# Two-block decoder layer on one core: S5 states two tokens a step, placed between the mLSTM heads, with the projections in the same block

## The chip, the core and the metric

The kernel runs on one core of a Trainium2 chip. The time is device microseconds (us) from the first to the last instruction of one execution, with what lies around it. Engines: TensorE (PE) does matmuls, VectorE (DVE), ScalarE (ACT) and GpSimd (POOL) do elementwise work, SyncE (SP) issues the DMAs. Each runs its own list of instructions in order, and they wait for each other by semaphores.

## The reference

Two blocks are applied to 256 tokens of width 1024. The first (a hybrid mixer and a gated feed-forward) isn't touched. The second puts 16 meta tokens ahead (272 tokens), and computes, cut to what matters:

```python
xn = rmsnorm(h, norm1_g)
u_s, x_m, z_m, g_s, g_m = split(xn @ w_in)          # 512, 1024, 1024, 1024, 1024 columns
# S5: 32 groups of 16 channels and 64 complex states
a_bar = exp(lam * dt);  b_bar = (a_bar - 1) / lam * b
s[t] = a_bar * s[t-1] + b_bar @ u[t]                # written as an associative scan
y = gelu(real(c @ s) + d * u);  y = y * sigmoid(y @ w_glu + b_glu)
# mLSTM: 4 heads of 256
xc = silu(conv4(x_m));  q, k = blockdiag(xc);  v = blockdiag(x_m)
log_i, log_f = gates(q, k, v)
hm = sum_s(w_ts * (q_t . k_s) * v_s) / max(|den|, exp(-m))     # w_ts = exp of gate sums, s <= t
hm = sigmoid(z_m) * hm;  hm = hm * rsqrt(mean(hm ** 2) + eps) * norm_g + skip * xc
h = h + (sigmoid(g_s) * (y @ w_ssm_out) + sigmoid(g_m) * (hm @ w_ml_out)) @ w_out
```

A retrieval of experts (PEER) and a final norm follow.

## The kernel before

Activations lie as channels on 128 partitions by tokens (T = 256, or TT = 272 with the M = 16 meta tokens). Weights come in blocks of 128 x 1024 (512 KB) through a ring of 8 SBUF slots: SP loads them in the order of `stream` (`load`, line 159), each waiting until PE has counted its slot `used`. `project` (PE) and `evacuate` (ACT or DVE) go through them by PSUM bank: PE waits for `full[slot]` and `drained[bank]`, the reader for `used[slot]`. A weight and its input that need precision are split into a rounded high part and a low part (`part_high` on ACT, line 248; `part_low`, line 252) and take three matmuls (`three`, lines 257 to 259). Others are plain f32 matmuls (line 228). A block (`nc.Block`) ends with all engines waiting for each other.

The middle of the second block is two such blocks, lines 1204 to 1258 and 1308 to 1690.

The first does 12 blocks of projection for u_s and x_m: PE three matmuls by eight chunks each (`product`), ACT the high parts and the reading of the banks (line 1251), DVE the low parts. POOL copies x.

The second goes, by PE's list: 2 z products (a z product is one weight block of the 24 for z_m, g_s and g_m, 8 matmuls of 256 columns, read by ACT, line 1299); v (lines 1609, 1615); 2 z products; q and k (line 1623), which wait for the SiLU of the convolution (DVE lines 1336 to 1340, ACT line 1550); 4 z products; the gate sums (line 1630); 2 z products around the row operations of the gates on DVE (lines 1383 to 1396) and ACT; the four heads; the head norms; then the S5 states.

A head: PE spreads rows of gate sums over partitions (lines 1648, 1649) and forms scores (line 1653) and one z product; DVE adds the columns (lines 1403 to 1407), ACT takes exp, DVE multiplies (1410, 1411); PE forms the weighted sums and denominator (line 1664); DVE divides (lines 1416 to 1420) and counts `head_read`, for which the next head on PE waits. After the four heads DVE multiplies by sigmoid(z) and squares all of them (1423, 1425), PE sums (1670), DVE takes one reciprocal of 1024 columns (1430), ACT its root (1574), and DVE 16 steps of gain and skip (1433, 1435).

The S5 states are 16 groups of 128 complex states by 272 tokens, handled in 8 pairs. A complex recurrence becomes two real ones when the inputs are turned by exp(-i theta t): DVE turns (lines 1448 to 1453), scans with the real factor r (line 1461), and POOL and DVE turn back (lines 1513 to 1521, 1464). PE makes a pair's inputs (line 1696), ACT copies them to SBUF (line 1581), and PE sums the outputs (lines 1685, 1686) with a z product for each pair. The tables cos and sin of theta t are made on POOL by doubling, from one angle (lines 1492 to 1502), through the gate and head stages. The last pairs have part of POOL's work on DVE (`SHARED`). Then y on DVE (line 1472), a sigmoid of all gates (line 1585) and the gelu (line 1590) on ACT end the block. The mix stage (from line 1724 on) follows with its own block; its first weights are loaded ahead by SP, at the end of its list in this block.

## Time and profile before

| | |
|---|---|
| median of 3 runs | 1919.95 us (1916.93 to 1920.94) |
| profiled execution | 1916.86 us, span 1915.1 us |
| busy share | PE 89%, DVE 63%, ACT 41%, POOL 23% |
| mean granted TensorE clock | 0.935 |

The page gives averages over a program with several stages; the change touches the stretch from 623 to 957 us. For such a stretch one reads the busy sums by stage and then the timeline of each engine, where a bracket says how long the engine was idle before an instruction and what ended that. A matmul in f32 appears as two records. A granted clock of 1.0 is 2.4 GHz and of 0.5 is 1.2 GHz; in between it is a mean over the stretch. A z product is 16 records of 256 columns.

### The profile page before, as it was taken

To read this page: it belongs to the slowest core of one execution; us is meant where nothing else is said; L and a number is where in the kernel's file an instruction comes from. 1 tells how busy PE (TensorE), PEld (TensorE's weight loads), DVE (VectorE), ACT (ScalarE), POOL (GpSimd) and SP (SyncE) were. 2 spreads that over 40 slices of the span, in tenths; PEclk is the share of its full clock that TensorE was granted. 3 is DMA by queue.
4 is the path that set the end of the run, shared out by engine and by line. 5 is a ranking of instruction groups with operands and counts; after the bars stand their busy time and mean duration, and the time that the engine had idled before them with its cause. 6 is when DMAs were issued, how large, how long until landed. Compare 5 with 4: busy or idle time off the path is not lost. (4 is left out here: it accounts for less than half of the span.)

```text
span 1915.1 us, 32548 instructions
## 1 busy us (share of the span) xinstructions
PE 1698.7 (89%) x10946; PEld 1514.3 (79%) x10946; DVE 1213.2 (63%) x2250; ACT 781.5 (41%) x1330; POOL 444.1 (23%) x355
## 2 busy tenths in 40 slices
PE   5988999779995887777495999899999999999997
PEld 5967987669995874554285999899999988888886
DVE  4374214667776352379844599877777467777776
ACT  3441113045552342011232455455555555555554
POOL 0020001214441049206572779500000000000000
PEclk9989999889997898787697999999999999999999
DMA  6412224235552521011143467655555776766663
GB/s 229 154 33 89 77 87 156 66 122 184 183 186 72 200 67 55 22 55 66 44 143 100 133 214 214 199 178 177 176 175 180 231 239 232 242 230 230 236 236 131
DMA packets 93698, 289.40 MB, mean 151 GB/s; under 512 B 11328, under 2 KB 27968, under 8 KB 93248
## 3 DMA queue, kind: packets, MB, share of 16 engines
q1 hardware_dynamic: 93200, 287.61, 45.4%
q10 hardware_dynamic: 432, 0.90, 0.2%
q8 instruction: 42, 0.69, 0.1%
q14 instruction: 24, 0.20, 0.0%
HBM read 270.64 MB, written 17.83 MB: 151 GB/s over the span
## 5 line engine op out<-in xcount | busy, mean ns | idle before, releaser
L257 PE MATMUL bank<-arena_parts 128*128 128x256 f32 (+2 forms) x1664 | 482.2, 290 | 62.2 <-DVE ring_parts L252 23.5
L259 PE MATMUL bank<-arena_parts,ring_parts 128*128 128x256 f32 (+1 forms) x1600 | 454.7, 284 | 0.0
L2297 DVE TENSOR_TENSOR ring_parts<-ring,arena_parts 128x512 fp32r<-128x512 f32 x434 | 293.3, 689 | 131.1 <-ACT arena_parts L2117 104.3
L257 PEld LDWEIGHTS bank<-arena_parts 128*128 128x128 f32 x1664 | 319.7, 192 | 67.2 <-issue 20.1
L258 PE MATMUL bank<-h_parts,arena_parts 128*128 128x256 f32 x1152 | 324.1, 281 | 0.0
L259 PEld LDWEIGHTS bank<-arena_parts,ring_parts 128*128 128x128 f32 x1600 | 307.5, 192 | 0.0
L252 POOL TENSOR_TENSOR ring_parts<-ring,arena_parts 128x1024 fp32r<-128x1024 f32 x79 | 208.6, 2657 | 296.8 <-ACT arena_parts L248 242.9
L258 PEld LDWEIGHTS bank<-h_parts,arena_parts 128*128 128x128 f32 x1152 | 218.1, 189 | 0.0
L228 PE MATMUL bank<-h,ring 128*128 128x256 f32 x896 | 213.8, 398 | 1.0 <-PEq L1203 1.0
L2086 PE MATMUL bank<-arena_parts,x_parts 128*128 128x512 f32 x512 | 202.9, 396 | 2.7 <-DVE x_parts L2324 2.7
L228 PEld LDWEIGHTS bank<-h,ring 128*128 128x128 f32 x896 | 177.8, 202 | 33.1 <-issue 7.8
L2088 PE MATMUL bank<-arena_parts,x_parts 128*128 128x512 f32 x512 | 202.7, 396 | 0.0
L2087 PE MATMUL bank<-ring_parts,x_parts 128*128 128x512 f32 x512 | 200.9, 392 | 0.0
L2117 ACT ACTIVATE arena_parts<-ring 128x512 fp32r<-128x512 f32 x217 | 136.5, 629 | 124.1 <-PE bank L2088 96.8
L2114 ACT ACTIVATE arena_parts<-ring 128x512 fp32r<-128x512 f32 x217 | 136.6, 630 | 73.1 <-PE bank L2088 58.7
L258 PE MATMUL bank<-arena_parts 128*128 128x256 f32 (+1 forms) x448 | 130.5, 291 | 0.0
L1016 DVE TENSOR_TENSOR ring_parts<-ring,arena_parts 128x1024 fp32r<-128x1024 f32 x66 | 84.8, 1289 | 51.8 <-ACT arena_parts L1011 47.2
L2086 PEld LDWEIGHTS bank<-arena_parts,x_parts 128*128 128x128 f32 x512 | 95.7, 187 | 25.6 <-DVE ring_parts L2297 2.9
L2087 PEld LDWEIGHTS bank<-ring_parts,x_parts 128*128 128x128 f32 x512 | 96.3, 188 | 23.8
L2088 PEld LDWEIGHTS bank<-arena_parts,x_parts 128*128 128x128 f32 x512 | 95.7, 187 | 24.1
L248 ACT ACTIVATE arena_parts<-ring 128x1024 fp32r<-128x1024 f32 x76 | 79.2, 1053 | 58.0 <-DMA ring<-stream 58.0
L1050 PE MATMUL bank<-arena_parts 128*128 128x256 f32 x352 | 100.3, 285 | 2.9 <-DVEq L1100 2.9
(461 smaller groups left out, 3051.4 us busy)
## 6 DMA issues: line engine op xcount, KB each, us to landing
ring<-stream SPq DMA_DIRECT2D x473, 512.0 KB, 3.5
kept<-arena SPq DMA_DIRECT2D x128, 128.0 KB, 2.1
arena<-kept SPq DMA_DIRECT2D x32, 512.0 KB, 4.5
arena<-first SPq DMA_DIRECT2D x1, 2144.0 KB, 8.1
arena<-second SPq DMA_DIRECT2D x1, 1632.0 KB, 7.2
x<-x_t SPq DMA_DIRECT2D x1, 1024.0 KB, 5.8
out<-arena SPq DMA_DIRECT2D x4, 256.0 KB, 2.1
arena<-last ACTq DMA_DIRECT2D x1, 512.0 KB, 3.4
```

Source lines behind the costliest of these rows:

```text
L228: mm = nc.tensor.matmul(b[:, 0:width], w[:, k, :], h[:, k, lo:lo + width], start=k == 0, stop=k == KT - 1)
L252: ns.tensor_tensor(low[:, s, :], ring[:, s, :], high[:, s, :].bitcast(F32), ALU.subtract)\
L257: nc.tensor.matmul(dst, stationary[0], moving[0], start=first, stop=False)
L258: nc.tensor.matmul(dst, stationary[0], moving[1], start=False, stop=False)
L259: return nc.tensor.matmul(dst, stationary[1], moving[0], start=False, stop=last_one)
L1050: mm(b, high[:, s, w], h_high[:, k, :], start=k == 0, stop=False)
L2086: mm(b, gate_high[:, q % 4, t], expert_high[:, m % 2, w], start=False, stop=False)
L2087: mm(b, gate_high[:, q % 4, t], low[:, s, w], start=False, stop=False)
L2088: ins = mm(b, gate_low[:, q % 4, t], expert_high[:, m % 2, w], start=False, stop=last_one)
L2114: nc.scalar.activation(expert_high[:, m % 2, halves[0]], ring[:, s, halves[0]], ACT.Copy)\
L2117: nc.scalar.activation(expert_high[:, m % 2, halves[1]], ring[:, s, halves[1]], ACT.Copy)\
L2297: v.tensor_tensor(low[:, s, w], ring[:, s, w], expert_high[:, m % 2, w].bitcast(F32), ALU.subtract)\
```

## The change

- **One block.** The projections and what follows share a block. The stream has the columns of x_m ahead of those of u_s. The loops are unrolled, DVE makes a channel's convolution after each low part from the fifth block on, ACT a SiLU from the seventh on.
- **Two tokens a step.** The recurrence runs over pairs of tokens: 136 columns instead of 272, with the factor r squared and the angle doubled. PE forms each pair's input as A B u (first token) + B u (second), accumulated in PSUM, which DVE now reads directly. Outputs of one kind of token are C times the state, of the other C A times the state before plus K0 u, K0 = C B by group. A B, C A and K0 are made once: spread copies of A (PE), products (DVE), transposes of B (PE), 32 small matmuls and four copies for K0. The outputs are written to every second column of bank 1.
- **Tables by sines.** DVE multiplies theta by a ramp of 136, takes whole turns off, and ACT takes sin, and cos as 1 - 2 sin^2 of the half. POOL's doubling goes.
- **Norms folded.** Each head is gated, squared (ACT) and summed (PE) at once, and division and norm become one factor 1 / sqrt(mean(hg^2) + eps den^2), with one reciprocal of 256 columns per head. Gain and skip are applied during the next head.
- **Woven.** Each head holds two pairs of states; POOL turns back all eight pairs apart from one product in DVE. The z products go 2, 1, 2, 1, 1, 1, then two in each head, 2 and 6 at the end, the last eight read by ACT with sigmoid.

The core of the diff:

```diff
+        psum = ctx.enter_context(nc.psum_tensor("psum", [P, 8 * 512], F32))
+        bank = [psum[:, i * 512:(i + 1) * 512] for i in range(8)]
         ident, ones, iota = cst[:, 0:P], cst[:, P:2 * P], cst[:, 2 * P:3 * P]
...
+        def z_bank(g):
+            return g % 2 if g < 8 else 0 if g < 16 else g % 2 * 2
...
-                sp.wait_ge(S("second_in"), 16)
-
-            @block.gpsimd
-            def _(pool):
-                poo.link(nc.gpsimd.tensor_copy(x[:], xin[:, :, M:TT]))
-
...
+                poo.tell(g.tensor_copy(x[:], xin[:, :, M:TT]), x_kept, ONCE + 1)
+                for p in range(PAIRS):
+                    cs, sn = er[:, 2 * p:2 * p + 2, CT - OT - 1:CT], ei[:, 2 * p:2 * p + 2, CT - OT - 1:CT]
+                    zr, zi = zt[:, p % 2, 0:2, CT - OT - 1:CT], zt[:, p % 2, 2:4, CT - OT - 1:CT]
+                    pool.wait_ge(S("z_ready"), p + 1)
+                    if p >= 2:
+                        pool.wait_ge(S("c_done"), p - 1)
+                    so, st = s_out[p % 2], s_tmp[p % 2]
+                    poo.link(g.tensor_tensor(so[:, 0], zr, cs, ALU.mult))
+                    poo.link(g.tensor_tensor(st[:, 0], zi, sn, ALU.mult))
+                    poo.link(g.tensor_tensor(so[:, 0], so[:, 0], st[:, 0], ALU.subtract))
+                    poo.link(g.tensor_tensor(so[:, 1], zr, sn, ALU.mult))
+                    poo.tell(g.tensor_tensor(so[:, 1], so[:, 1], st[:, 1], ALU.add), S("s_ready"), p + 1)
...
+                for n in range(12):
+                    part_low(dve, nc.vector, xn_block, n % 4, split["blocks"] + n + 1)
+                    if n >= 4:
+                        conv(n - 4)
...
+                v.tensor_copy(ramp[:, 0:P], iota)
+                v.tensor_scalar(ramp[:, P:CT], iota[:, 0:CT - P], float(P), None, ALU.add)
+                vec.link(v.tensor_tensor(sm(S_TH2), sm(S_TH), sm(S_TH), ALU.add))
+                vec.link(v.tensor_tensor(ei, ramp.unsqueeze(1).broadcast_to([P, 16, CT]),
+                                         sm(S_TH2).unsqueeze(2).broadcast_to([P, 16, CT]), ALU.mult))
+                turn_k, angle = (t.rearrange("p s t -> p (s t)") for t in (er, ei))
+                vec.link(v.tensor_scalar(turn_k, angle, 1.0 / TWO_PI, 12582912.0, ALU.mult, ALU.add))
+                vec.link(v.tensor_scalar(turn_k, turn_k, 12582912.0, None, ALU.subtract))
+                vec.link(v.scalar_tensor_tensor(angle, turn_k, -6.28125, angle, ALU.mult, ALU.add))
+                vec.link(v.scalar_tensor_tensor(angle, turn_k, -0.0019353071795864769, angle, ALU.mult, ALU.add))
+                vec.tell(v.tensor_scalar(angle, angle, 3.1415925, -3.1415925, ALU.min, ALU.max), table_angles, ONCE + 1)
...
+                def rotate(p):
+                    dve.wait_ge(S("bu_done"), p + 1)
+                    cs, sn = er[:, 2 * p:2 * p + 2, :], ei[:, 2 * p:2 * p + 2, :]
+                    xr, xi = (rot[:, n, :].rearrange("p (s t) -> p s t", s=2) for n in range(2))
+                    q0, q1 = (rt[:, n, :].rearrange("p (s t) -> p s t", s=2) for n in range(2))
+                    v.tensor_tensor(q0, bu_im, sn, ALU.mult)
+                    real = step(v.tensor_tensor(xr, bu_re, cs, ALU.mult))
+                    v.tensor_tensor(q1, bu_re, sn, ALU.mult)
+                    v.tensor_tensor(xi, bu_im, cs, ALU.mult).then_inc(S("bu_turned"), 1)
+                    dve.wait_ge(vec.steps, real)
+                    step(v.tensor_tensor(xr, xr, q0, ALU.add))
+                    dve.wait_ge(S("bu_turned"), p + 1)
+                    vec.link(v.tensor_tensor(xi, xi, q1, ALU.subtract))
+                def scan(p):
+                    if p >= 2:
+                        dve.wait_ge(S("s_ready"), p - 1)
+                    for s in range(2):
+                        r = sm(S_R2)[:, 2 * p + s:2 * p + s + 1].broadcast_to([P, CT])
+                        for c in range(2):
+                            xx = rot[:, c, s * CT:(s + 1) * CT]
+                            ins = v.tensor_tensor_scan(zt[:, p % 2, 2 * c + s, :], r, xx, 0.0, ALU.mult, ALU.add)
+                    vec.link(ins)
+                    vec.tell(v.tensor_tensor(s_tmp[p % 2][:, 1], zt[:, p % 2, 2:4, CT - OT - 1:CT],
+                                             er[:, 2 * p:2 * p + 2, CT - OT - 1:CT], ALU.mult), S("z_ready"), p + 1)
...
+                    if hh:
+                        finish_head(hh - 1)
+                    rotate(2 * hh)
...
+                    scan(2 * hh)
                     dve.wait_ge(S("head_sums"), hh + 1)
...
+                    if hh == 0:
+                        dve.wait_ge(S("z_sigmoid"), 1)
+                    vec.tell(v.tensor_tensor(h_ml[:, 2 * hh:2 * hh + 2, :], b3(4), zsig[:, 2 * hh:2 * hh + 2, :], ALU.mult),
+                             head_gated, ONCE + hh + 1)
+                    vec.link(v.tensor_scalar(rd, bank[5][:, 0:T], -1.0, None, ALU.mult))
+                    vec.link(v.tensor_tensor(rd, rd, bank[5][:, 0:T], ALU.max))
+                    vec.tell(v.tensor_tensor(rd, rd, bank[5][:, T:2 * T], ALU.max), head_den, ONCE + hh + 1)
...
+                    rotate(2 * hh + 1)
+                    scan(2 * hh + 1)
+                    if hh:
+                        finish_y(hh - 1)
+                    dve.wait_ge(squares_den, ONCE + hh + 1)
+                    dve.wait_ge(S("ml_sums"), hh + 1)
+                    vec.tell(v.scalar_tensor_tensor(root_h, bank[4][:, 0:T], 1.0 / T, rd, ALU.mult, ALU.add),
+                             S("head_read"), hh + 1)
+                    vec.tell(v.reciprocal(root_h, root_h), S("ml_inverse"), hh + 1)
+                finish_head(3)
+                finish_y(3)
...
+                act.wait_ge(table_angles, ONCE + 1)
+                cos_t, sin_t = (t.rearrange("p s t -> p (s t)") for t in (er, ei))
+                sca.link(a.activation(cos_t, sin_t, ACT.Sin, scale=0.5))
+                a.activation(sin_t, sin_t, ACT.Sin)
+                sca.link(a.activation(cos_t, cos_t, ACT.Square))
+                sca.tell(a.activation(cos_t, cos_t, ACT.Identity, scale=-2.0, bias=ones[:, 0:1]), S("tables"))
+                z_reads(act, 3)
...
+                    act.wait_ge(head_gated, ONCE + hh + 1)
+                    a.activation(hsq, h_ml[:, 2 * hh:2 * hh + 2, :], ACT.Square).then_inc(S("ml_squares"), 1)
+                    act.wait_ge(head_den, ONCE + hh + 1)
+                    a.activation(rd, rd, ACT.Square, scale=RMS_EPS ** 0.5).then_inc(squares_den, 1)
                     z_reads(act, 1)
+                    act.wait_ge(S("ml_inverse"), hh + 1)
+                    a.activation(root_h, root_h, ACT.Sqrt).then_inc(S("ml_root"), 1)
...
+                z_reads(act, 2, ACT.Sigmoid)
                 for b in range(2):
                     act.wait_ge(drained[b], ev_at.banks[b] + 1)
-                sca.link(a.activation(zg[:, 8:24, :].rearrange("p c t -> p (c t)"),
-                                      zg[:, 8:24, :].rearrange("p c t -> p (c t)"), ACT.Sigmoid))
-
-                nc.scalar.activation(spare[:], ones[:, 0:1], ACT.Gelu_apprx_tanh)
-                act.wait_ge(S("s5_y"), 1)
+                gates_read_first = zg[:, 8:16, :].rearrange("p c t -> p (c t)")
+                sca.link(a.activation(gates_read_first, gates_read_first, ACT.Sigmoid))
+                z_reads(act, 6, ACT.Sigmoid)
...
+                for j in range(16):
+                    c, r = j // 4, slice(32 * (j % 4), 32 * (j % 4) + 32)
+                    dst = bank[4][r, 32 * c:32 * c + 32]
+                    mm(dst, bt_re[:, c, r], c_re[:, j, :], start=True, stop=False)
+                    ins = mm(dst, bt_im[:, c, r], c_im[:, j, :], start=False, stop=True)
+                ins.then_inc(k0_made, 1)
...
+                def inputs(p):
+                    if p:
+                        pe.wait_ge(S("bu_turned"), p)
+                    for s in range(2):
+                        j = 2 * p + s
+                        c, r = j // 4, slice(32 * (j % 4), 32 * (j % 4) + 32)
+                        for k, (b, b_a) in enumerate(((b_re, ab_re), (b_im, ab_im))):
+                            dst = bank[6 + s][:, k * CT:(k + 1) * CT]
+                            mm(dst, b_a[r, c, :], even[r, c, :], start=True, stop=False)
+                            ins = mm(dst, b[r, c, :], odd_[r, c, :], start=False, stop=True)
+                        if s == 0:
+                            turn(pe, ins)
+                    ins.then_inc(S("bu_done"), 1)
+                def outputs(p):
+                    c = p // 2
+                    dst = y_bank.rearrange("p (k s) -> p s k", s=2)
+                    if p % 2 == 0:
+                        if c:
+                            pe.wait_ge(y_taken, ONCE + c)
+                        mm(dst[:, 0, :], k0[:, c, :], even[:, c, M // 2:CT], start=True, stop=False)
+                    pe.wait_ge(S("s_ready"), p + 1)
+                    for s in range(2):
+                        j = 2 * p + s
+                        r = slice(32 * (j % 4), 32 * (j % 4) + 32)
+                        for k, m in enumerate((ca_re, ca_im)):
+                            mm(dst[r, 0, :], m[:, j, :], s_out[p % 2][:, k, s, 0:OT], start=False, stop=k == 1)
+                        for k, m in enumerate((c_re, c_im)):
+                            ins = mm(dst[r, 1, :], m[:, j, :], s_out[p % 2][:, k, s, 1:OT + 1], start=k == 0, stop=k == 1)
+                    ins.then_inc(S("c_done"), 1)
...
+                    inputs(2 * hh)
                     z_products(pe, 1)
...
+                        outputs(2 * hh - 1)
+                    inputs(2 * hh + 1)
+                    z_products(pe, 1)
+                    pe.wait_ge(S("ml_squares"), hh + 1)
+                    for c in range(2):
+                        ins = mm(bank[4][:, 0:T], ones, hsq[:, c, :], start=c == 0, stop=c == 1)
+                    ins.then_inc(S("ml_sums"), 1)
+                    outputs(2 * hh)
...
+                outputs(PAIRS - 1)
+                z_products(pe, 6)
...
+    parts += [_blocks(w_in2[:, 512:1536]), _blocks(w_in2[:, :512])]
```

## Rows read from the trace of the kernel before

**Rows 1.** The page: granted clock in 40 slices; stream loads, us to landing.
```profile
PEclk9989999889997898787697999999999999999999
...
ring<-stream SPq DMA_DIRECT2D x473, 512.0 KB, 3.5
```
**Rows 2.** Stretches: length, then per engine busy us (count), clock, DMA share, GB/s.
```profile
623.00:668.00 45.00, 38.25 (x288) 38.04 (x288) 17.55 (x15) 15.39 (x23) 1.89 (x1) 0.88 0.58 201
668.00:748.50 80.50, 67.73 (x314) 51.20 (x314) 35.02 (x80) 31.47 (x62) 50.39 (x122) 0.92 0.22 72
748.50:823.60 75.10, 62.88 (x219) 42.92 (x220) 23.94 (x40) 5.76 (x15) 31.00 (x34) 0.79 0.09 28
823.60:850.00 26.40, 16.61 (x55) 12.11 (x53) 20.28 (x22) 3.06 (x5) 0.00 (x0) 0.74 0.12 40
850.00:957.00 107.00, 66.64 (x234) 41.26 (x232) 97.60 (x96) 20.31 (x45) 59.21 (x36) 0.72 0.16 59
```
**Rows 3.** Timeline, DVE in the states: start, duration, engine, line, shapes, count.
```profile
851.15 0.73 DVE L1448 TENSOR_TENSOR arena<-arena 128x544 f32<-128x544 f32 x1 [1.51 <-ACT arena L1581]
...
861.53 1.67 DVE L1450 TENSOR_TENSOR arena<-arena 128x544 f32<-128x544 f32 x1
...
868.34 2.57 DVE L1461 TENSOR_TENSOR_SCAN arena<-arena 128x272 f32<-128x272 f32 x4
```
**Rows 4.** Timeline, PE in the states and at the mix stage; idle and releaser in brackets.
```profile
857.10 2.42 PE L1696 MATMUL bank<-arena 32*128 32x272 f32 x8
...
867.78 1.07 PE L1685 MATMUL bank<-arena 128*32 128x256 f32 x4 [4.61 <-POOL arena L1521]
...
930.97 0.63 PE L1685 MATMUL bank<-arena 128*32 128x256 f32 x4 [1.45 <-POOL arena L1521]
931.43 0.61 PE L1686 MATMUL bank<-arena 128*32 128x256 f32 x4
...
957.34 2.90 PE L1738 MATMUL bank<-arena,ring 128*128 128x256 f32 x6 [3.50 <-PEq L1308]
```
**Rows 5.** Timeline, PE and DVE in the second head.
```profile
767.64 1.22 PE L1648 MATMUL bank<-arena 4*128 4x256 f32 x2 [4.01 <-DVE arena L1420]
...
769.64 4.42 PE L1653 MATMUL bank<-arena 128*16 128x256 f32 x12
...
777.58 3.02 PE L1664 MATMUL bank<-arena 128*128 128x256 f32 x12
780.53 1.54 PE L1664 MATMUL bank<-arena,cst 128*128 128x256 f32 x6
...
785.33 0.69 DVE L1420 TENSOR_TENSOR arena<-bank,arena 128x512 f32<-128x512 f32 x1
```
**Rows 6.** Timeline, DVE in the norm stage and ACT at the end.
```profile
833.59 6.55 DVE L1430 RECIPROCAL arena<-arena 128x1024 f32<-128x1024 f32 x1
...
934.95 1.28 ACT L1588 ACT_TABLE_LOAD   x1
...
955.66 1.06 ACT L1590 ACTIVATE arena<-arena 128x1024 f32<-128x1024 f32 x1 [19.21 <-DVE arena L1472]
```
**Rows 7.** Timeline, DVE: a convolution, gate rows, one pass of the norm stage.
```profile
671.75 1.57 DVE L1340 SCALAR_TENSOR_TENSOR arena<-arena,par 128x271 f32<-128x271 f32 x3
...
740.51 1.46 DVE L1391 TENSOR_TENSOR arena<-arena 4x272 f32<-4x272 f32 x1
...
746.26 0.43 DVE L1396 TENSOR_TENSOR arena<-arena 4x272 f32<-4x272 f32 x1
...
825.96 2.29 DVE L1425 TENSOR_TENSOR arena<-arena 128x2048 f32<-128x2048 f32 x1
```
**Rows 8.** Timeline, PE from the block's start to the gates.
```profile
668.27 7.14 PE L228 MATMUL bank<-h,ring 128*128 128x256 f32 x32 [1.00 <-PEq L1203]
...
697.22 9.89 PE L1623 MATMUL bank<-arena,ring 128*128 128x272 f32 x32 [4.45 <-ACT arena L1550]
...
720.85 11.17 PE L1630 MATMUL bank<-arena 128*8 128x272 f32 x48
```

521 lines of the change are left out of this document (229 added, 292 removed).

## Prediction, made from the kernel before alone

> **What bounds the kernel now.** I read the slices of the page first. TensorE (PE) has 6 to 9 tenths almost everywhere, but in slices 14 to 20 the granted clock falls to between 6 and 9 tenths [rows 1]: the second block's middle, which is what the change rewrites. Then the stretches from 623 to 957 us [rows 2], each with its busy sums. The first, 623 to 668, is the 12 projections, bound by PE. In the next three PE is busy for 147 of 182 us at clocks of 0.92, 0.79 and 0.74. The last, 850 to 957, is the S5 states: DVE is busy for 97.60 of 107 us and PE for 66.64, much of that stretched by a clock of 0.72. So PE bounds the start, DVE the end, and hand-overs between engines the middle.
>
> The timelines say why. In the states each DVE product with two SBUF inputs takes 1.67 us, against 0.73 for the one that ran with POOL idle; POOL's own take 1.64 each (59.21 / 36 [rows 2]); the scans (2.57 for four) are not touched [rows 3]. A pair costs DVE 97.6 / 8 = 12.2 us. PE then waits 4.61 us for POOL, and its next products take 1.07 us where those behind 1.45 us took 0.63 [rows 4]. In a head PE waits 4.01 us for DVE; ten records' worth of 256 columns then take 4.42 us [rows 5], 0.44 a record; 32 such records in a row take 7.14 at full clock, 0.215 each with the last one's drain [rows 8]. These are the 1.2 and the 2.4 GHz level; a matmul is two records. In the norm stage one reciprocal of 1024 columns takes 6.55 us, with PE waiting [rows 6].
>
> The sum is a walk in trace time from the end of the projections to the start of the mix stage (957.3), which starts 0.6 us after a gelu of 1.06 us ends at 956.7 [rows 6].
>
> **Part 1, one block with the projections.** PE's 12 projections are unchanged. The x_m columns now come first, so DVE makes the convolutions beside them. One channel is three steps of 1.57 us in all [rows 7] and a shorter one, 2.1 with its gaps, and a low-part subtraction 1.2 (DVE's 17.55 us in 15 operations [rows 2]). That is 3.3 us against PE's 3.0 a block for the last eight; the subtractions fall 2.5 us behind and had over 3 us in hand, so I cost it at nothing. If that cover is missing, PE waits about 1 us. ACT adds a SiLU of 0.35 us a block to some 1.5. The barrier (1.00 us) and the wait for SiLU (4.45 us) go [rows 8]. POOL has only its copy and a memset; SP's queue of loads is the same without a break.
>
> PE: start 667.3; two z products 7.1 (674.4); v products, 10.3 by subtraction in rows 8 (697.22 - 4.45 - 668.27 less twice 7.1); one z 3.5 (688.2); q and k 9.7 (697.9), though they are held some 2 us by ACT's sines, whose reads then come faster; eight new transposes, 16 records of half that width at 0.115, 1.9 (699.8); two z 7.1 (706.9); gates 11.2 [rows 8] (718.1). Before, the gates ended at 732.0: 13.9 us earlier, 10.5 of which is only z products moved behind.
>
> **Part 2, tables by sines.** 81 us of POOL work up to 782 go (50.39 + 31.00 [rows 2]); it did not end last, but of DVE's row operations on 4 x 272 one took 1.46 us beside its long products and one 0.43 beside its short ones [rows 7]. DVE adds six passes over 2176 columns; one of 2048 took 2.29 [rows 7], so at most 2.43 each, 14.6 in all, from 672 to 687; then the sines, 41 small ones and two groups of C products, 14 us, to about 704. It waits for PE until 718, so all this is covered by 14 us. ACT adds four passes; 1024 columns took 1.06 [rows 6], so 2.2 each, from 700 to 709, and delays z reads that PE needs only at 718.
>
> Then, to the heads: copy 0.5, z 3.5 beside it, split 1.2 (722.8); DVE 1.6; ACT two table loads of 1.28 [rows 6] and 1.0 (728.0); DVE's six row operations, now uncontended, 3.4 (731.4). PE meanwhile: z 3.5 (726.3), spreading A 1.9 (728.2), and K0. **K0 is not in the trace**: 32 tiny matmuls, 64 records. Bounds: 0.06 us each (half of an output record's 0.46 / 4 = 0.115, the moving side being an eighth [rows 4]) is 3.8; 0.23 (the gates' narrow records, 11.17 / 48 [rows 8]) is 14.9. I take 0.115, the nearest in shape (32 output columns), 7.4 (735.6). Columns 1.2 and z 3.5 follow (740.3), beside DVE's A*B products, 6 x 0.7. Heads start at 740.5, not 748.5. Gain 8 us; 11.6 or 0.5 at the bounds.
>
> **Part 3, the woven heads.** Per head at full clock PE has: selection 0.43, scores 2.15, inputs of a pair 2.4 [rows 4], z 3.45, selection 0.43, sums 4.45 [rows 5], outputs 1.3, inputs 2.4, z 3.45, squares 0.9, outputs 1.3. Sum 22.7. The widths at 0.215 for 256; the sums are 777.58 to 782.07; an output group is four records of 0.46 twice, and drain. Inputs are 8 matmuls of 136 columns for 4 of 272, the same columns; outputs likewise.
>
> DVE: logs 1.3; norm of the head before 2.1; rotation 2.8 (six of 0.43; four read PSUM, where no slowing shows: 0.69 for 512 columns at 785.33 with one such source [rows 5]); weights 1.1; scans 1.5 and product 0.4 (half of 2.57 and 0.69 with a fixed part); gating and denominator 2.1; rotation and scans again 4.7; y 0.5; reciprocal 1.75 (a quarter of 6.55 [rows 6] and a fixed part) and a multiply 0.5. Sum 18.7, under PE. With three SBUF products per pair stretched by 0.5, 21.7, still under.
>
> What ends last: from the scores' end DVE's logs, ACT's exp behind a table load (2.2), the old norm, the rotation and the weights end at 7.4 us. PE, with inputs and z, is at the wait for them at 6.0: idle 1.4. Sums end at 12.3; DVE's rotation can start at once when the second inputs end at 16; PE's z and squares end at 20.5, but its next outputs wait for `y_taken`, which DVE tells at 21.3: idle 0.8. The reciprocal (to 23.6) and ACT's root lie beside the next scores. So the period is 22.7 + 1.4 + 0.8 and 0.6 for hand-overs: 25.5. A gap of 1.45 us left the clock up in the states; gaps of 4.01 and 4.61 did not [rows 4, 5]. Behind PE's waits for squares and for y stand the next scores; behind DVE's wait for the sums stands the second pair.
>
> Four heads: 102 us, to 842.5. They hold the 75.1 of heads, the 26.4 of norms and the 107 of states of before [rows 2].
>
> **Part 4, the tail.** Two z 7.1, last outputs 1.3, six z 20.7: 871.6, with ACT making sigmoids as it reads. Then a read 0.4, the gelu with its table load, now not ahead, 1.28 + 1.06 [rows 6]: 874.4, and 0.6 for the block's end: 875.0. The mix stage's loads now issue only at 871.6; landing takes 3.5 us [rows 1] and the first of these slots is wanted by ACT 2 us after the stage starts, so nothing or 1 us.
>
> **Sum:** 957.3 - 875.0 = 82.3 us. The profiled execution took 1916.86 (span 1915.1), the median of the runs is 1919.95, 3.1 higher. 1916.9 - 82.3 = 1834.6; on the median 1837.7. I say **1838**. All else is as before.
>
> The Trainium skill, "SBUF — State Buffer", section "Door 1: The DMA port swizzle", says that PSUM has 8-byte cachelines and that any non-contiguous PSUM pattern significantly slows matmuls. The outputs now write every second float of the bank. No row here shows such a write.
>
> **Rivals.**
> (a) *Strided outputs.* Outputs write each second column. As a mechanism of this kernel: all 9.6 us of outputs and K0's quarter double, +10 us, 1848; at four times, +30, 1868. For: no row has it. Against: a record of 256 columns takes four passes' time, so writes come slowly (0.215 us). Chance 0.1.
> (b) *The clock does not hold.* If hand-overs in a head sum to 6 us in one or two gaps, PE pays 4 us of half clock after each, as at [rows 4, 5]: period 32, +26, 1864. It decides once one gap exceeds 4 us. For: ACT has four table switches a head. Against: PE has z products between waits. 0.15.
> (c) *The weave is serial* (the slower side). If each engine waits out the others, a head costs 22.7 + 18.7 + 5.7 of ACT (two table loads 2.6, passes 3.1) = 47, +86, 1924. The point is the wait for weights and the wait for squares: both would have to hold with no second work queued. 0.03; between this and (b) another 0.02 within 0.2%.
> (d) *Better than that:* K0 at its low bound (-3.6) and no idle (-11): 1823. 0.1.
> (e) *The change is no weave at all*, the z products at the end being what PE's gaps held before: then only DVE's halved states (about -45) count, 1875. Against: the PE sum shows it is full. 0.03.
>
> **How the numbers follow.** Forecast 0.57, 1828 to 1852 by K0's bounds and 3 us a head. The range 1820 to 1868 takes in (a), (b) and (d); about 0.1 to 0.2 lies outside. A measurement can tell about 0.2% from no change. Faster 0.95, same 0.02, slower 0.03.
>
> **What would show it.** Right: q and k start near 688, gates end near 718; DVE rows about 0.45 us; heads at 740; four head periods of 25 to 26 us with clock near 1.0 and PE over 90% busy; eight z products after the heads; mix stage at 875. Wrong: K0 over 12 us, outputs over 2 us, a PE gap over 2 us in a head, the clock under 0.9 there, or a mix stage that waits for its weights.

## The result, and the profile after

The changed kernel takes **1824.07 us** (median of four runs, 1822.69 to 1825.87), against 1920.45 (1916.93 to 1921.92) for the kernel before: a ratio of 0.9503, 95% interval 0.9488 to 0.9517. The forecast was 1838, the range 1820 to 1868; the result lies below the 1828 to 1852 that the forecast itself was given, in the part that rival (d) had. The profiled execution took 1822.69 us, its span is 1820.9.

The page of the changed kernel: granted clock in 40 slices, as in [rows 1].
```profile
PEclk8989899889999699899979999999999999999999
```
From 637 to 865 us, slices 15 to 19, it reads 9, 9, 8, 9 and 9 tenths; in the kernel before, slices 16 to 20 had 8, 7, 8, 7 and 6. The 6 of slice 14 (592 to 637) is the norm, which ends with a wait of 12.8 us on PE, and the block's start at 624.5.

The windows of the changed kernel: length, then busy us (count) of PE, PE's weight loads, DVE, ACT, POOL, clock, DMA share, GB/s. They are the projections, the v to gate products, the woven heads and the tail, and answer to [rows 2].
```profile
624.50:662.50 38.00, 37.99 (x289) 38.00 (x290) 27.74 (x43) 14.94 (x25) 0.00 (x0) 0.95 0.53 192
662.50:724.50 62.00, 61.01 (x370) 46.40 (x369) 34.06 (x71) 38.21 (x66) 0.00 (x0) 1.00 0.20 70
724.50:827.70 103.20, 102.12 (x529) 77.79 (x528) 63.16 (x147) 24.37 (x37) 27.73 (x38) 0.93 0.13 46
827.70:860.70 33.00, 29.59 (x146) 25.45 (x145) 3.05 (x6) 9.08 (x14) 1.51 (x3) 1.00 0.40 153
```
PE is busy for 230.7 of 236.2 us. In the kernel before, from its first product (629.0) to the mix stage (957.3), it was busy for 252.1 of 328.3 [rows 2, 4]. So of the 92.1 us that went, 70.7 are PE's idle time, and 21.4 are busy time, since fewer products run at half the clock.

The timeline of the changed kernel: PE from the first z product to the mix stage.
```profile
662.32 7.07 PE L229 MATMUL psum<-h,ring 128*128 128x256 f32 x32
...
681.96 7.50 PE L1670 MATMUL psum<-arena,ring 128*128 128x272 f32 x32
689.30 1.04 PE L1675 MATMUL psum<-cst,arena 128*128 128x128 f32 x8
...
718.36 0.28 PE L1703 MATMUL psum<-arena 128*32 128x32 f32 x7
...
718.99 0.23 PE L1704 MATMUL psum<-arena 128*32 128x32 f32 x3
720.21 0.73 PE L1708 MATMUL psum<-cst,arena 4*16 4x4 f32 x6 [0.99 <-DVE arena L1426]
...
724.52 0.69 PE L1751 MATMUL psum<-arena 4*128 4x256 f32 x2
...
740.58 5.41 PE L229 MATMUL psum<-h,ring 128*128 128x256 f32 x16
...
827.73 7.17 PE L229 MATMUL psum<-h,ring 128*128 128x256 f32 x32
...
860.69 8.83 PE L1821 MATMUL psum<-arena,ring 128*128 128x256 f32 x32 [3.41 <-PEq L1274]
```
The whole of K0 (L1703 and L1704, in turns) lies between 718.36 and 719.2. The heads run from 724.52 to 827.73. The z product at 740.58 took 5.41 us where one at full clock takes 3.72, with no idle time ahead of it: the surprise of this case.

DVE's and POOL's steps in the first head, against [rows 3]:
```profile
731.64 0.43 DVE L1454 TENSOR_TENSOR arena<-arena 128x272 f32<-128x272 f32 x1
...
733.50 1.44 DVE L1466 TENSOR_TENSOR_SCAN arena<-arena 128x136 f32<-128x136 f32 x4
...
735.55 0.73 POOL L1301 TENSOR_TENSOR arena<-arena 128x258 f32<-128x258 f32 x1 [114.66 <-DVE arena L1468]
```
A pair's addition fell from 1.67 us to 0.43: with POOL quiet the kernel before took 0.73 for 544 columns [rows 3], and half the columns make that 0.43. POOL's own products fell from 1.64 to 0.73, with 258 columns instead of 512 and no product of DVE beside them.

### The profile page after: what moved, and what is told of

Read it like the earlier page. It is cut to its first block and busy times, and to the rows that moved or that the text cites. A ratio compares the mean times of both kernels' runs of the same rounds, so it can differ in the third digit from the quotient of the medians.

```text
span 1820.9 us, 32801 instructions
## 1 busy us (share of the span) xinstructions
PE 1677.4 (92%) x11170; PEld 1517.9 (83%) x11170; DVE 1152.2 (63%) x2268; ACT 794.7 (44%) x1326; POOL 333.6 (18%) x205
## 5 line engine op out<-in xcount | busy, mean ns | idle before, releaser
L258 PE MATMUL psum<-arena_parts 128*128 128x256 f32 (+2 forms) x1664 | 483.3, 290 | 59.9 <-DVE ring_parts L253 24.1
L260 PE MATMUL psum<-arena_parts,ring_parts 128*128 128x256 f32 (+1 forms) x1600 | 455.6, 285 | 0.0
L258 PEld LDWEIGHTS psum<-arena_parts 128*128 128x128 f32 x1664 | 320.8, 193 | 64.3 <-issue 29.0
L259 PE MATMUL psum<-h_parts,arena_parts 128*128 128x256 f32 x1152 | 325.2, 282 | 0.0
L260 PEld LDWEIGHTS psum<-arena_parts,ring_parts 128*128 128x128 f32 x1600 | 308.5, 193 | 0.0
L259 PEld LDWEIGHTS psum<-h_parts,arena_parts 128*128 128x128 f32 x1152 | 219.4, 190 | 0.0
L229 PE MATMUL psum<-h,ring 128*128 128x256 f32 x896 | 212.2, 397 | 0.0
L2169 PE MATMUL psum<-arena_parts,x_parts 128*128 128x512 f32 x512 | 202.9, 396 | 2.7 <-DVE x_parts L2407 2.7
L2171 PE MATMUL psum<-arena_parts,x_parts 128*128 128x512 f32 x512 | 202.7, 396 | 0.0
L2170 PE MATMUL psum<-ring_parts,x_parts 128*128 128x512 f32 x512 | 200.9, 392 | 0.0
L2169 PEld LDWEIGHTS psum<-arena_parts,x_parts 128*128 128x128 f32 x512 | 95.7, 187 | 25.9 <-DVE ring_parts L2380 2.9
L2171 PEld LDWEIGHTS psum<-arena_parts,x_parts 128*128 128x128 f32 x512 | 95.7, 187 | 24.1
```

Of the source, the lines that this page charges most:

```text
L229: mm = nc.tensor.matmul(b[:, 0:width], w[:, k, :], h[:, k, lo:lo + width], start=k == 0, stop=k == KT - 1)
L258: nc.tensor.matmul(dst, stationary[0], moving[0], start=first, stop=False)
L259: nc.tensor.matmul(dst, stationary[0], moving[1], start=False, stop=False)
L260: return nc.tensor.matmul(dst, stationary[1], moving[0], start=False, stop=last_one)
L2169: mm(b, gate_high[:, q % 4, t], expert_high[:, m % 2, w], start=False, stop=False)
L2170: mm(b, gate_high[:, q % 4, t], low[:, s, w], start=False, stop=False)
```

## The experiments

The base of each is the changed kernel. "Heads" is the time from the first head's first product to the tail. All the kernels share the code ahead of the block, and its first product falls between 623.52 and 629.64 us in them; where two traces are compared, it is therefore from that product. Behind the mix stage's start the kernels share their code too, and still differ by up to 4 us at one place there (the section on the prediction has it), so the causes are read from the block.

**1. The pairs behind the heads.** Is it the weaving that gained?
```
 for hh in range(4):
-    inputs(2 * hh) ... outputs(2 * hh - 1); inputs(2 * hh + 1) ... outputs(2 * hh)
-z_products(pe, 2); outputs(PAIRS - 1); z_products(pe, 6)
+for p in range(PAIRS):
+    inputs(p); z_products(pe, 1)
+    if p: outputs(p - 1)
+outputs(PAIRS - 1)
```


> The pairs of states come after the four heads instead of inside them; the eight z products of the tail go between them, one to a pair. Every operation is kept. Theory A (PE is the bound, and only its products count once the z products lie between the waits): in a head DVE's logs 1.3, ACT's exponential 1.1 and the weights 1.0 with the old norm's 1.7 stand against one z product of 3.7, so PE waits about 1 us a head; a pair has 7.3 us of PE (2.4 + 3.7 + 1.3) against 4.1 of DVE and 4.0 of POOL, so no wait, but the last pair's chain (rotation 2.1, scans 1.9, POOL 4.0) is open by about 3 us and the gelu stands behind it: in all 5 to 10 us over the changed kernel, 1829 to 1834. Theory B (the weaving itself is what gained, since a pair's chain of DVE and POOL or a head's chain can only be hidden by the other): 4 us of waits at each of the four heads and at pairs, with half clock behind each: 30 us or more over, 1855 and up.

Measured: 1823.99 us (1823.55 to 1825.51), ratio 0.9509 (0.9488 to 0.953). The same as woven. Its windows, PE alone, heads and then pairs:
```profile
725.30:790.90 65.60, 64.22 (x280) 1.00 0.19 64
790.90:861.00 70.10, 68.21 (x395) 0.90 0.24 86
```
PE waits 1.4 us in four heads and 1.9 in eight pairs. From first product to mix stage it is 237.95 us against 236.18. One z product in each wait does all that the weave does. Theory A's mechanism holds; of the 5 to 10 us that it priced, 1.8 show in the block and none in the median.

**2. DVE's state work twice.** Did halving it matter?
```
+v.tensor_tensor(q0, ...) ... (the six steps of rotate once more)
-for s in range(2):
+for again in range(2):
+    for s in range(2):
```


> Each rotation and each scan is made twice, so that DVE has per pair about what states of one token at a time would give it, uncontended: 3.7 us more a pair, 7.4 a head, 30 in all. Theory A (DVE is off the path in the woven heads; its waits in a head sum to about 9 us): 0 to 5 us over the changed kernel, 1824 to 1829, with DVE's waits shorter by some 7 us a head. Theory B (halving DVE's work is what made the weave fit): DVE becomes the bound, 15 to 30 us over, 1839 to 1854.

Measured: 1855.11 us (1848.34 to 1859.82), ratio 0.9676 (0.965 to 0.9703): 31 us over, so theory A falls. (The profiled execution is the fastest of the four, 25.7 over the changed kernel's.) The heads' window:
```profile
725.50:857.70 132.20, 118.30 (x530) 88.06 (x529) 93.35 (x227) 24.37 (x37) 27.80 (x38) 0.82 0.11 36
```
Two of PE's waits in the second head, from the timeline, for the weights (the step at L1509) and for y (L1481):
```profile
763.19 0.69 PE L1772 MATMUL psum<-arena 4*128 4x256 f32 x2 [2.35 <-DVE arena L1509]
...
780.82 0.49 PE L1744 MATMUL psum<-arena 128*128 128x128 f32 x2 [2.41 <-DVE arena L1481]
```
Yet theory B's reason is not what the row shows either: DVE is busy for 93 of 132 us and so is not the bound. PE waits 13.9 us in all, mostly for the weights and for y, ahead of which the rotation stands on DVE, and the clock falls to 0.82. Of 29.0 us in the heads, 12.8 are waits, and 16.2 slower products.

**3. Twice the DVE work, with the pairs behind the heads.** Order or amount? The edits of 1 and 2 together.

> Each rotation and scan is made twice, as before, but with the pairs of states behind the heads instead of inside them. Theory A (the 31 us that twice the DVE work cost in the weave came from its order: the rotation stands ahead of the weights and of y, PE waits 2.4 us there and then runs at half clock): a pair has 7.3 us of PE at full clock, and from its inputs to its outputs lie 10.7 us of PE's other work against a chain of 11.7 (rotation 4.4, scans 3.3, POOL 4.0); about 1 us of wait a pair and 3.7 more at the last: 5 to 15 us over the unwoven kernel, 1829 to 1839. Theory B (DVE's amount of work is what counts, wherever it lies): 25 to 35 us over, 1849 to 1859.

Measured: 1843.56 us (1842.68 to 1845.27), ratio 0.9617 (0.9597 to 0.9636): 19.6 us over the unwoven kernel, between both theories. The pairs' window, PE alone:
```profile
791.40:875.00 83.60, 67.08 (x392) 0.90 0.22 82
```
The last pair's outputs, from the timeline:
```profile
873.13 1.06 PE L1749 MATMUL psum<-arena 128*32 128x128 f32 x4 [7.59 <-POOL arena L1305]
```
PE waits 16.5 us in the pairs against 1.9, 7.59 of them for the last pair. From first product to mix stage the doubling costs 14.2 us here (252.18 against 237.95) and 29.0 in the weave (265.23 against 236.18). So half of what it costs in the block comes with the amount, wherever it lies, and half with its place in the weave; the medians (19.6 of 31) also hold differences behind the mix stage's start. Halved state work did matter, not because DVE was full, but because a pair's chain through DVE and POOL must fit beside PE's products.

**4. z products ahead of the inputs.** Meant for the clock:
```
-inputs(2 * hh); z_products(pe, 1)
+z_products(pe, 1); inputs(2 * hh)
 ...
-inputs(2 * hh + 1); z_products(pe, 1)
+z_products(pe, 1); inputs(2 * hh + 1)
```


> In each head both z products come before the pair's input products instead of behind them. In the changed kernel four of eight z products behind inputs ran at half clock for some 3.5 us with no idle time ahead of them, which cost about 7 us. Theory A (the products with 32 rows are what let the clock fall, whatever follows): all z products take 3.72 us, and the half clock strikes the sums and squares that now follow the inputs; cost about the same 7 us. Theory B (the clock falls with something else, DVE's or POOL's work or a fixed interval): half-clock stretches are found again inside z products. For the time: the rotation ahead of the weights starts 3.5 us later, so PE waits up to 3 us for the weights in each head: 0 to 13 us over the changed kernel, 1824 to 1837.

Measured: 1879.4 us (1878.15 to 1882.27), ratio 0.98 (0.9777 to 0.9822): 55 us over, far outside what either theory gave. The heads' window, PE alone:
```profile
726.30:880.40 154.10, 129.65 (x529) 0.71 0.09 31
```
PE's waits for the weights and for y in the second head:
```profile
771.84 1.21 PE L1765 MATMUL psum<-arena 4*128 4x256 f32 x2 [3.31 <-DVE arena L1502]
...
794.88 0.80 PE L1737 MATMUL psum<-arena 128*128 128x128 f32 x2 [3.56 <-DVE arena L1474]
```
PE waits 24.5 us: 3.3 for each head's weights, as I expected, and 3.4 to 3.7 in three heads for `y_taken`, which I had not seen. Of the 50.9 us that the heads are longer, these waits are 23.4 more than before, and 27.5 are slower products. Both theories on the clock meet a trace with too many gaps to tell them apart.

**5. The same first half, with the weights made before the rotation.**
```
-inputs(2 * hh); z_products(pe, 1)
+z_products(pe, 1); inputs(2 * hh)
 ...
-rotate(2 * hh)
 (DVE's two weights steps)
+rotate(2 * hh)
```


> In the first half of each head the z product comes ahead of the pair's inputs, as in the kernel that put z first, but DVE makes the head's weights ahead of the rotation; the second half stays. Theory A (what cost 55 us there were the waits for weights and for y that a later rotation made, and the half clock behind them): no wait for the weights, since they are ready 5.5 us after the scores against 6.0 of PE's own work; 0 to 4 us under the changed kernel, 1820 to 1824, by fewer half-clock stretches. Theory B (a z product ahead of the inputs is itself what hurts): 15 us or more over, 1839 and up.

Measured: 1843.64 us (1842.91 to 1843.93), ratio 0.9614 (0.9595 to 0.9633): 19.6 us over. The heads' window, PE alone, then the second head in pieces:
```profile
725.40:846.40 121.00, 120.26 (x529) 0.75 0.13 40
...
760.00:762.00 2.00, 1.94 (x18) 1.00 0.44 137
762.00:764.00 2.00, 2.00 (x9) 0.58 0.34 133
764.00:766.00 2.00, 2.00 (x6) 0.50 0.00 0
...
780.00:782.00 2.00, 2.00 (x6) 0.50 0.00 0
782.00:784.00 2.00, 2.00 (x9) 0.80 0.00 0
```
The waits are gone (0.7 us in 121), as theory A said, and still it loses 17.8 us in the heads. None of it is waiting, so what is left is the clock: from 762.3 to 782.8 PE works without a gap at 1.2 GHz. It falls just behind the inputs at 759.66, in the sums: 5.39 us where 3.02 is full clock.

**6. No states.**

> The states are left out of the weave: no input products, rotation, scans, POOL products, outputs or sum y; the tables and scaled matrices are still made, and gelu takes what the projections left. Theory A (the states cost what PE's products of them take, 3.7 us a pair, and the half clock behind them): a head falls from 25.8 us to about 16, with PE waiting under 1 us for weights; 8 x 3.7 and 7 us of clock, 37 us under the changed kernel, 1787. Theory B (the states lie in gaps that the heads leave anyway): 10 us or less under. If the half-clock stretches come with the 32-row products, none is left in the heads.

Measured: 1788.08 us (1787.33 to 1789.14), ratio 0.9321 (0.93 to 0.9341): 36 us under, theory A's 37. The heads, PE alone:
```profile
729.60:795.50 65.90, 64.52 (x281) 1.00 0.19 64
```
103.2 - 65.9 = 37.3 us. The work of DVE and POOL on the states is hidden; that of PE is not: the states cost what PE needs for them, and the half clock. The clock is 1.00 throughout.

**7. Inputs on all rows.** The cause of the clock:
```
-mm(dst, b_a[r, c, :], even[r, c, :], start=True, stop=False)
-ins = mm(dst, b[r, c, :], odd_[r, c, :], start=False, stop=True)
+mm(dst, b_a[:, c, :], even[:, c, :], start=True, stop=False)
+ins = mm(dst, b[:, c, :], odd_[:, c, :], start=False, stop=True)
```


> The input products take all 128 rows of the weights and of the moving side instead of one group of 32, with the same columns and count; the sum then runs over four groups, so the states computed are not the reference's. Theory A (products on 32 of the 128 rows are what lets the granted clock fall while PE is never idle): every z product behind inputs takes 3.72 us, none 5.41; 7 us less, 1817. Theory B (the clock falls with PE's columns or with something outside PE): episodes at half clock as before, 1824.

Measured: 1820.91 us (1819.4 to 1821.16), ratio 0.9492 (0.9469 to 0.9515), whose interval overlaps the changed kernel's. The trace is clear where the time isn't; the heads' window, PE alone:
```profile
726.50:823.90 97.40, 94.20 (x530) 1.00 0.16 49
```
The clock is 1.00 in all the heads, though PE is idle for 3.2 us there instead of 1.1, and no z product takes over 3.62. Heads: 97.4 against 103.2. Of these 5.8 us, 2.35 are lost behind the mix stage's start, where its first products took 9.94 us instead of 8.83 and the next 5.41 instead of 3.72. Theory A holds for the cause, and some of the gain is given back later. What changed is the form of the products: whether it is the rows at work or something else that comes with 32-row products can't be told from this, but the zeros of the last kernel below show that it isn't the data.

**8. POOL busy as before.**
```
+for _ in range(24):
+    poo.link(g.tensor_tensor(st, so, so, ALU.mult))
```


> POOL makes 24 products of 516 columns that nobody reads, from 684 us on, where the kernel before made its tables by doubling. Two of 258 columns take 0.73 us each with DVE quiet, so 24 of 516 take some 35 to 40 us and end near the heads' start (724). Theory A (POOL's work slows DVE's products with two SBUF sources, and of those the gate rows and the A*B products lie on the path): the gate rows' two-source steps go from 0.43 to 1.46 us, the last two A*B products from 0.69 to 1.6; the C products slow too but are hidden in DVE's wait of 12.6 us; heads start 3 to 5 us later: 1827 to 1829. Theory B (the slow steps of before had another cause): nothing moves, 1824.

Measured: 1824.39 us (1821.15 to 1826.27), ratio 0.9516 (0.9493 to 0.9539): no change. POOL, then two of DVE's C products, then a gate row, from the timeline:
```profile
683.98 31.10 POOL L1298 TENSOR_TENSOR arena<-arena 128x516 f32<-128x516 f32 x24
...
693.56 1.53 DVE L1404 TENSOR_TENSOR arena<-arena 128x512 f32<-128x512 f32 x1
695.01 1.53 DVE L1405 TENSOR_TENSOR arena<-arena 128x512 f32<-128x512 f32 x1
...
716.90 0.43 DVE L1426 TENSOR_TENSOR arena<-arena 4x272 f32<-4x272 f32 x1
```
A C product takes 0.68 us with POOL quiet and 1.53 beside it, all hidden in DVE's wait of 12.6 us for the gates. The load ended at 715.1, before the gate rows, so theory A's price on the path wasn't tried, and my estimate of when POOL ends was 9 us late. What is shown is that POOL's company is enough for the factor of 2.3 in [rows 3] (1.67 against 0.73): here it is 2.25.

**9. Convolutions after the projections.**
```
     part_low(...)
-    if n >= 4:
-        conv(n - 4)
+for n in range(8):
+    conv(n)
```


> DVE makes the eight convolutions after the last low part instead of beside the projections, and ACT its SiLUs beside the v products; there is still one block. Theory A (what made the front shorter is the order of the products, v ahead of q and k, and the convolutions would have been in time anyway): they end at about 677 us, five ahead of q and k at 682; tables and C products 15 us later, still ahead of the gates at 708: 0 to 1 us, 1824 to 1825. Theory B (the convolutions beside the projections removed the 4.45 us that PE waited for SiLU before): 4 us or more, 1828 and up.

Measured: 1824.86 us (1823.22 to 1830.02), ratio 0.9523 (0.9495 to 0.955). The last convolution and the start of q and k, from the timeline:
```profile
672.52 1.57 DVE L1325 SCALAR_TENSOR_TENSOR arena<-arena,par 128x271 f32<-128x271 f32 x3
...
684.50 7.50 PE L1667 MATMUL psum<-arena,ring 128*128 128x272 f32 x32
```
The convolutions end at 674.1, 10 us before q and k. These start 58.7 us behind the first product instead of 57.5. So the convolutions beside the projections only add slack, as theory A says. But its reason, v ahead of q and k, can't be what took the 4.45 us off [rows 8]: v stood there in the kernel before too. Its timeline, the last convolution on DVE and then ACT:
```profile
686.19 1.57 DVE L1340 SCALAR_TENSOR_TENSOR arena<-arena,par 128x271 f32<-128x271 f32 x3
...
692.81 0.38 ACT L1299 ACTIVATE arena<-bank 128x256 f32<-128x256 f32 x1 [3.07 <-PE bank L228]
694.50 2.67 ACT L1550 ACTIVATE arena<-arena 128x272 f32<-128x272 f32 x8
```
The convolutions were done at 687.8, 9.5 us ahead of q and k. The SiLUs came so late since they stood in ACT's list behind the reads of two z products, and the second of these ended on PE only at 692.8; a table load of 1.28 us and the eight SiLUs lay open behind it. The changed kernel has them ahead of its first z read, this experiment has them beside the reads of v. Both leave ACT's order changed, so no run tries it alone.

**10. Contiguous outputs.**
```
-dst = y_bank.rearrange("p (k s) -> p s k", s=2)
+dst = y_bank.rearrange("p (s k) -> p s k", s=2)
```


> The outputs write the even and the odd tokens of a channel group as two contiguous halves of the PSUM bank instead of every second float, and the step that takes y reads the bank with the stride. Theory A (a write with a stride of two floats costs PE nothing here): a group of 16 output records takes the same 1.46 us, no change, 1824. Theory B (strided PSUM writes are slower): a group takes less, by up to half; 8 x 0.7 is 6 us, 1818.

Measured: 1822.59 us (1822.0 to 1823.68), ratio 0.9505 (0.9482 to 0.9527), the changed kernel's ratio. The first products of an output group and the first behind it, from the timelines, here and in the changed kernel:
```profile
746.60 0.62 PE L1744 MATMUL psum<-arena 128*32 128x128 f32 x4
...
748.06 0.69 PE L1752 MATMUL psum<-arena 4*128 4x256 f32 x2
...
747.00 0.62 PE L1743 MATMUL psum<-arena 128*32 128x128 f32 x4
...
748.46 0.69 PE L1751 MATMUL psum<-arena 4*128 4x256 f32 x2
```
The 16 records take 1.46 us, and with the stride 1.46 too. Theory A. The Trainium skill ("SBUF — State Buffer", "Door 1: The DMA port swizzle") has non-contiguous PSUM patterns slow matmuls significantly; in these f32 products at a stride of two floats, the trace does not show it.

**11 and 12. Two attempts at a faster version.** The first, on top of the edits of experiment 5:
```
 if hh: outputs(2 * hh - 1)
+z_products(pe, 1)
 inputs(2 * hh + 1)
 ...
-ins = mm(bank[6 + n][:, o], a_spread[:, n, o], ident, start=True, stop=True)
+ins = nc.tensor.transpose(bank[6 + n][:, o], a_spread[:, n, o], ident)
 ...
-z_reads(act, 6, ACT.Sigmoid); (gelu)
+(gelu); z_reads(act, 2, ACT.Sigmoid)
```


> An attempt at a faster version. To the order with the weights first come: a third z product in each head, between the outputs of one pair and the inputs of the next (four fewer in the tail); y taken ahead of the second rotation; the gelu ahead of ACT's last two reads of z; and the spread of A's rows by transposes instead of products with the identity. By the traces: full-row products stand between every two stretches of 32-row ones, so the half-clock stretches (6 to 7 us in the changed kernel) go; gelu with its table load no longer stands between the last product and the mix stage, 2.3 us; the transposes take 1.0 us instead of 1.95. In all 10 us under the changed kernel, 1814. If the half clock comes regardless of the order, 1821; if the gelu's table loads now hold up the last reads, 1 or 2 us more.

Measured: 1825.15 us (1818.33 to 1828.01), ratio 0.9511 (0.949 to 0.9532): nothing gained. PE ahead of the heads, from the timeline:
```profile
722.84 0.99 PE L1708 MATMUL psum<-cst,arena 4*16 4x4 f32 x6 [1.91 <-DVE arena L1426]
723.76 6.78 PE L229 MATMUL psum<-h,ring 128*128 128x256 f32 x16
```
The heads' window, PE alone:
```profile
730.50:847.40 116.90, 116.44 (x593) 0.91 0.18 57
```
The transposes saved 0.9 us that PE then waits for DVE's gate rows (1.91 instead of 0.99), and the z product behind ran at half clock, 3.1 us more, though no 32-row product stood ahead of it. Two heads had a half-clock stretch of some 10 us each, the other two none (27.2 us with three z products). The order of full-row products alone does not keep the clock up.

The second takes the rows instead, with a moving side that POOL fills into zeroed buffers:
```
+ins = g.tensor_copy(masked[r, j % 4, :], us[r, p // 2, :])
 ...
-mm(dst, b_a[r, c, :], even[r, c, :], start=True, stop=False)
+mm(dst, b_a[:, c, :], masked_two[:, j % 4, 0, :], start=True, stop=False)
```


> A second attempt at a faster version, in the order of the changed kernel. The input products take all 128 rows with the reference's result: POOL copies the 32 rows of u that a product needs into one of four buffers that are zero elsewhere, two copies of 32 x 272 a pair, and the products take that as their moving side. With it the gelu ahead of ACT's last four reads of z and A's rows by transposes. Theory A (the clock follows how many rows are at work): no half clock in the heads, 6 us as in the kernel with full rows, of which 2 go again to a longer half-clock stretch at the mix stage; 2.3 for the gelu and 0.9 for the transposes: 7 us under the changed kernel, 1817. Theory B (the zeros count as no work, so the clock falls as with 32 rows): 1821, with the half-clock stretches in z products as before.

Measured: **1817.06 us** (1815.75 to 1822.09), ratio 0.948 (0.9461 to 0.9499): 7.0 us under the changed kernel by the medians, where 7 were expected; by the ratios, each against the kernel before on its own chip, 4.4 us (0.0023 of 1920), and their intervals overlap. So it is likely faster, not shown to be. Windows of heads and tail, all engines:
```profile
726.00:823.30 97.30, 94.10 (x529) 72.63 (x528) 63.17 (x147) 24.39 (x37) 32.59 (x50) 1.00 0.15 49
823.30:855.30 32.00, 29.62 (x146) 25.48 (x145) 2.97 (x6) 10.40 (x15) 1.82 (x3) 1.00 0.42 143
```
Theory A: rows that hold zeros keep the clock up as well. The other terms came out otherwise. The transposes again cost, 1.7 us up to the heads, and again by the clock of the z product behind them:
```profile
720.76 5.29 PE L229 MATMUL psum<-h,ring 128*128 128x256 f32 x16
```
The early gelu gave 1.0 of its 2.3: between ACT's last step and its first of the next block now lie 1.79 us instead of 0.46. The timeline of SyncE's queue has what ends the block instead: when PE's last product is done, at 852.92, SP issues its last four loads, the first of which waits for a ring slot that PE holds, and is done with them at 854.67; the next block begins at 855.10. In the changed kernel the same four lay beside the gelu. And the mix stage started at full clock (7.14 us instead of 8.83), which gave back what the transposes took.

## Why the prediction was right, and where its sizes were not

The mechanism was right: PE's products are the bound of the whole block, and each wait has something of PE's beside it. The number was further off: 13.6 us of 1838, below the 1828 to 1852 that was given 0.57, and nearest to a rival given 0.1. By the forecast's own steps, from the first z product to the mix stage:

| step | forecast, us | measured, us |
|---|---|---|
| z, v, q and k, transposes, gates | 50.8 | 45.95 |
| gates' end to the heads | 22.4 | 16.25 |
| four heads | 102 | 103.2 |
| tail | 32.5 | 32.96 |

- **q and k** were sized at 9.7 from the 9.89 of [rows 8], which stood behind a wait of 4.45 us and so held products at 1.2 GHz. At full clock they take 7.34 (681.96 to 689.30): 2.4 us. The row was read, its clock wasn't. v took 9.3 for 10.3, since the subtraction had left a wait of 0.90 us for ACT in it (at 678.14 in the kernel before), and the transposes 0.9 for 1.9; only 8 records show, not the 16 that I counted.
- **K0** was sized at 7.4, with bounds of 3.8 and 14.9; it took 0.8, outside both: 64 records, 0.013 us apart. The row it was scaled from held the answer. An output record of [rows 4] has the same form, 128 rows on 32 columns of the array, and with 256 columns moved takes 0.115 us at a granted clock of 1.00; a full-width record of as many columns takes 0.215 [rows 8]. So products on different column groups already ran two at a time there. K0 moves an eighth of the columns, and an eighth of 0.115 is 0.0144, 0.92 us for 64 records. The forecast took the 0.115 whole, and half of it as its bound from below, as if a narrow product cost as much as a wide one. The Trainium skill ("TensorE: Matmul & The Clock Gate", "Part 3: Packing small matmuls — row/col tiling") has products on different groups of rows or columns run concurrently, and the trace agrees: a record of K0 lasts 0.20 us, and the next begins 0.013 behind it.
- **Heads**: 25.5 a head forecast, 25.8 measured, but from other parts. The idle of 2.2 us a head was 0.3 (1.1 in four heads); in its place stand 6.8 us of half clock in four z products, 5.41 instead of 3.72 each, and products of 23.8 us a head instead of 22.7 and 0.6 for hand-overs (a pair's outputs took 1.46 to 1.78 for 1.3). That the sum came out is luck: the misses cancelled.
- **DVE**: 18.7 us a head forecast, 15.8 measured (63.16 / 4). Rotation steps of 0.43, scans 1.44 and the reciprocal came as sized. That this DVE time was free was right; that it could be twice as much would have been wrong, by experiment 2.
- **Tables by sines, gate rows uncontended, the SiLU off the path**: all held (why the SiLU was on it before is under experiment 9). DVE's row steps took 0.43, and PE's wait for them was 0.99 us.
- **Outside the block**: the first product came 4.5 us sooner than in the kernel before, within the 6 us by which it lies apart in kernels that share that code; behind the mix stage's start 2.45 us more were spent. Its first products are not the reason: 32 records at half clock in both kernels, 9.09 us before and 8.83 after. Up to 1133 us the changed kernel is even 1.5 us ahead, counted from that start. It loses 3.9 at one place, from 1137.3 to 1144.1, where the granted clock is 0.50; the same products in the kernel before, from 1235.0 on, have 1.00. PE waited 1.19 and then 2.19 us around its start, where the kernel before has only the second wait, 2.18. Most of the experiments' kernels lose 1.4 to 4.0 us there, and three none (2, 4 and the first attempt), though all share that code; what decides it stays open. The median lies 1.4 above the profiled time, not 3.1.

The sum: 9.8 us too little taken off the projections and the block, 4.5 - 2.45 outside it and 1.7 for the median make the 13.6 between 1837.7 and 1824.1.

**The rivals.** (d), K0 at its low bound and no idle at 1823, is nearly the number that came, but not by its own terms: K0 lay 3.0 us under its bound, q and k and v gave 3.4 more, and the half clock took 6.8 back. (a), strided outputs, is refuted by experiment 10. (b), the clock, was right in part: 6.8 of its 26 us are paid, but not from gaps of 4 us as I wrote; none is in the heads. (c), the serial weave, is nowhere near; still, experiment 4 shows a reordering of two lines that costs 55 of its 86 us. (e), no weave at all, was given 1875 and 0.03: experiment 1 shows the weave itself is worth nothing, and that its price was wrong, because I counted only DVE's halved states and not the z products that PE has beside them in any order.

## What to carry to other kernels

Count the bound engine's products, and give each of its waits one of them; a fine weave on top gained nothing here, and an order inside it can cost 55 us. When a step is moved on PE, look at what stands behind it on the engine that answers (here DVE's rotation ahead of the weights and of y). When a duration is taken from a row, read the clock of that row first, and compare it with a row of full width before scaling it. Count products that use few rows of the array as a risk to the clock of whatever follows.

## What the runs showed of the hardware

- **The clock falls without a gap.** In experiment 5 PE is busy for 120.26 of 121.0 us at a mean clock of 0.75; with the states left out (clock 1.00) or the inputs on all 128 rows (1.00, with more idle time) it doesn't fall in the heads. Products of the same columns on 32 of 128 rows are what stood ahead of each fall there. The Trainium skill ("TensorE: Matmul & The Clock Gate", "Part 1: The HAM clock gate") gives the low level to an idle PE; here a busy one had it for 20 us. It is not the only way to lose it: in the two last kernels the z product ahead of the heads ran at half clock behind the transposes, K0 and a wait of 1.9 us, without any 32-row product, where the changed kernel, with a wait of 0.99, kept 1.00.
- **Zeros count.** Rows that carry zeros hold the clock like rows that carry data (1.00 in the heads of the last kernel).
- **How long it lasts** differed with what ran in it, which no run tries apart. With 32-row products inside it, it lasted 20.5 us (762.3 to 782.8, experiment 5); in the changed kernel, with a z product behind the inputs, 3.4 (741.3 to 744.7 by windows of 2 us).
- **Narrow products side by side.** On 32 columns of the array, a record of 256 moved columns took 0.115 us against 0.215 on all 128 [rows 4, 8], and one of 32 took 0.013.
- **DVE beside POOL**: 0.68 us becomes 1.53 for a product with two SBUF sources.
- **A stride of two floats in PSUM** cost nothing: 1.46 us for 16 records with and without.
